# Second recurrence: the small levels and the diagonal as 32x32 squares in four column groups, the 64-token level copied whole

## The reference, cut to what matters

```python
def step(state, inp):
    q_n, k_n, i_n, b_n = inp
    dec = jnp.exp(jnp.where(incl, b_n[:, :, :, None, :] - b_n[:, :, None, :, :], -jnp.inf))
    att = jnp.einsum('bhtd,bhsd,bhtsd->bhts', q_n, k_n, dec)
    o = (jnp.einsum('bhtd,bhdv->bhtv', q_n * jnp.exp(b_n), state)
         + jnp.einsum('bhts,bhsv->bhtv', att, i_n))
    ...
o_hf = _hgrn2_scan(qh, outs[0][0], ih, outs[0][1])
o_hb = _flip(_hgrn2_scan(_flip(qh), _flip(outs[1][0]), _flip(ih), _flip(outs[1][1])))
```

## Time and profile before

| | |
|---|---|
| time, three runs | 1533.93, 1534.42, 1536.74 us; median 1534.42 |
| span of the profiled execution, first to last instruction | 1535.2 us |
| busy: PE, PEld, DVE, ACT | 1508.5, 1403.2, 1200.7, 1015.8 us |
| share of the span: PE, DVE, ACT | 98%, 78%, 66% |
| chain that ended last: PE, DVE, ACT | 84%, 10%, 4% |
| mixer stretches in question | 122 to 182 us and 575 to 636 us |

### The profile page before, as it was taken

One profiled execution on the slowest core, in us unless ns is written; L12 is line 12 of the kernel. 1 busy time (PEld: TensorE's weight loads), 2 busy tenths in 40 slices (PEclk: granted clock), 3 DMA queues, 4 the chain that ended last, 5 costly groups with the idle time before them and its releaser, 6 DMA issues.

```text
span 1535.2 us, 29830 instructions
## 1 busy us (share of the span) xinstructions
PE 1508.5 (98%) x12702; PEld 1403.2 (91%) x12702; DVE 1200.7 (78%) x1693; ACT 1015.8 (66%) x1566; POOL 8.3 (1%) x18
## 2 busy tenths in 40 slices
PE   8999999999999999999999999999999998999998
PEld 8899999988889999999988889968999897899997
DVE  7999766889758799667898768875888578688864
ACT  7786865667646776765776546685777457677753
POOL 0000000000000000000000000000000001000000
PEclk9999999999999999999999999999999999999999
DMA  7522135555554422244655546402655543255551
GB/s 290 192 89 107 56 138 193 200 187 193 207 177 158 158 98 85 84 166 165 236 193 182 212 165 249 155 2 85 218 193 187 193 144 135 83 202 187 190 192 55
DMA packets 35700, 245.55 MB, mean 160 GB/s; under 512 B 4208, under 2 KB 4592, under 8 KB 6512
## 3 DMA queue, kind: packets, MB, share of 16 engines
q1 hardware_dynamic: 35568, 243.65, 44.3%
HBM read 242.58 MB, written 1.05 MB: 159 GB/s over the span
## 4 chain that ended last, share of the span: by engine, by line
PE 84%; DVE 10%; ACT 4%; DMA 1%; issue 1%; SPq 0%; DVEq 0%; ACTq 0%
PE PS L420 83%; DVE WL L1984 2%; DVE SB L1993 1%; DVE SB L1984 1%; DVE SA L1984 1%; ACT WH L1237 1%; ACT SB L1234 1%; DMA RAW<-w_in 1%; PE PS L423 1%; ACT SB L1911 1%; DVE SB L2259 1%; DVE SA L1993 0%; DVE SA L2161 0%; DMA X<-xt 0%; DVE SM L1984 0%
## 5 line engine op out<-in xcount | busy, mean ns | idle before, releaser
L420 PE MATMUL PS<-XHL,WH 128*128 128x256 f32 (+2 forms) x4080 | 846.8, 300 | 6.2 <-DVE WL L1984 3.5
L420 PEld LDWEIGHTS PS<-XHL,WH 128*128 128x128 f32 (+1 forms) x4080 | 644.8, 187 | 43.1 <-issue 5.6
L420 PE MATMUL PS<-XHL,WL 128*128 128x256 f32 (+1 forms) x2392 | 669.5, 280 | 0.0
L1237 ACT CAST WH<-RAW 128x2048 fp32r<-128x2048 f32 (+1 forms) x235 | 427.4, 1822 | 270.8 <-PE PS L420 259.0
L1984 DVE TENSOR_TENSOR WL<-RAW,WH 128x2048 fp32r<-128x2048 f32 (+1 forms) x235 | 511.9, 2181 | 113.2 <-ACT WH L1237 109.4
L420 PEld LDWEIGHTS PS<-XHL,WL 128*128 128x128 f32 (+1 forms) x2392 | 448.3, 187 | 0.4
L420 PE MATMUL PS<-INHL,WH 128*128 128x512 f32 (+1 forms) x1216 | 334.2, 344 | 0.0
L420 PE MATMUL PS<-INHL,WL 128*128 128x256 f32 x960 | 270.0, 281 | 0.0
L420 PEld LDWEIGHTS PS<-INHL,WH 128*128 128x128 f32 x1216 | 210.0, 188 | 27.6
L420 PEld LDWEIGHTS PS<-INHL,WL 128*128 128x128 f32 x960 | 181.2, 189 | 0.0
L1984 DVE TENSOR_TENSOR SB<-SB 128x512 f32<-128x512 f32 (+2 forms) x162 | 108.8, 674 | 14.5 <-ACT SB L1234 11.4
(11 more groups left out here) (156 smaller groups left out, 1446.0 us busy)
## 6 DMA issues: line engine op xcount, KB each, us to landing
RAW<-w_in SPq DMA_DIRECT2D x51, 1024.0 KB, 4.8
RAW<-w_up SPq DMA_DIRECT2D x44, 1024.0 KB, 4.8
RAW<-f_in SPq DMA_DIRECT2D x44, 1024.0 KB, 4.7
RAW<-w_down SPq DMA_DIRECT2D x22, 1024.0 KB, 4.8
RAW<-f_out SPq DMA_DIRECT2D x22, 1024.0 KB, 4.7
RAW<-a_w_in SPq DMA_DIRECT2D x10, 1024.0 KB, 5.0
RAW<-w_out SPq DMA_DIRECT2D x8, 1024.0 KB, 4.8
RAW<-w_bdn SPq DMA_DIRECT2D x4, 1024.0 KB, 4.8
```

The lines of the kernel that those rows point to most:

```text
L420: return e.matmul(out, l, r, start=start, stop=stop, skip_group_check=True)
L1237: e.copy(out, x).then_inc(*A.up(*key, of=of))
```

## The change: what it does

For levels 0 to 4 (g = 1 to 5) and for the diagonal, PE makes the four diagonal 32x32 squares of each unit in place of two 64x64 squares: 32 matmuls, 32 keys by 32 queries, to the four quarters of the PSUM partitions in turn (four column groups), in 256 columns of the bank. `attc` becomes 128x256. The masks of these levels are taken from a second place in the mask table. Level 5 (g = 6) is no longer merged under a mask by DVE: ACT copies its 64x64 squares whole from PSUM into `att`, waits for these copies, and then writes the four quarters of `attc` over the 32x32 squares on their diagonal.

```diff
-        attc = SB[:, 7168:7680].rearrange("p (m n) -> p m n", m=8)
+        attc = SB[:, 7168:7424].rearrange("p (m n) -> p m n", m=8)
+        def quarter_mask(lv):
+            return MKv[:, 2, lv, 64:96].unsqueeze(1).to_broadcast([128, 8, 32])
+        def own_quarter(q):
+            return attq[QUART[q], :, 0:4:3, QUART[q]]
...
                         h, s = divmod(m, 2)
+                        if lv < 5:
+                            for q in QUART:
+                                last = mm(p[q, m * 32:m * 32 + 32], zk[:, h, s, q], zq[:, h, s, q], True, True)
+                            continue
                         for b in range(2):
                             o = HALF[1 - b if lv == 6 else b]
...
-                        for o in HALF:
-                            last = mm(p[o, m * 64:m * 64 + 64], zv[:, h, s, o], qv[:, h, s, o], True, True)
+                        for q in QUART:
+                            last = mm(p[q, m * 32:m * 32 + 32], zv[:, h, s, q], qv[:, h, s, q], True, True)
...
-                    cp(attc, units(ps[st, "hgd"][:, :]), "diag", st, of=ps.out(st, "hgd"))
+                    cp(attc, units(ps[st, "hgd"][:, 0:256]), "diag", st, of=ps.out(st, "hgd"))
...
-                    w.wait_ge(*V["att", st])
+                    w.wait_ge(*P["ps", st, "hg", 6, 1])
                     for b in range(2):
-                        cp(own_square(b, b), heads(attc[HALF[b]]), "att", st)
+                        cp(own_square(b, b), heads(units(ps[st, "hg", 6, 1][:, :])[HALF[b]]), "squares", st, of=ps.out(st, "hg", 6, 1))
+                    waits(A["squares", st], V["att", st])
+                    for q in range(4):
+                        cp(own_quarter(q), heads(attc[QUART[q]]), "att", st)
...
-                    cpred(attc, level_mask(2, HGI[2 * g][1]), units(ps[st, "hg", g, 1][:, :]), "att", st, of=ps.out(st, "hg", g, 1))
+                    cpred(attc, quarter_mask(HGI[2 * g][1]), units(ps[st, "hg", g, 1][:, 0:256]), "att", st, of=ps.out(st, "hg", g, 1))
...
-                kept(6, after=5)
```

More of the change, by code:

```diff
@@ L289, in program @@
         HALF = (slice(0, 64), slice(64, 128))
+        QUART = [slice(32 * j, 32 * j + 32) for j in range(4)]
         att = SB[:, 11264:13312]
@@ L373, in program @@
         KKv = KK.rearrange("p (g n t) -> p g n t", g=4, n=2)
-        QUART = [slice(32 * j, 32 * j + 32) for j in range(4)]
         W2, MV = SA[:, 9472:9984], SA[:, 9984:10496]
@@ L3058, in constants @@
     r, c = np.arange(128)[:, None], np.arange(512)[None, :]
+    quarter = [mk[q:q + 32, 2, 0:5, q:q + 32].copy() for q in range(0, 128, 32)]
     for kind in range(3):
@@ L3061, in constants @@
             mk[64 * b:64 * b + 64, kind, :, 0:64] = mk[64 * b:64 * b + 64, kind, :, 64 * b:64 * b + 64]
+    for q in range(4):
+        mk[32 * q:32 * q + 32, 2, 0:5, 64:96] = quarter[q]
     mv = (r // 16 == 2 * (c // 128) + c % 128 // 64) & (r % 16 < 15)
```

## The result

The changed kernel takes 1537.36 us, the kernel before 1535.51 us in the same series (medians of 20 runs each): ratio 1.0014, interval 1.0008 to 1.0021. That is inside the 0.2% that the prediction called no change, but it is a loss of about 2 us where a gain of 0.4 was forecast, and just above the range. One run of the changed kernel took 5109.71 us and is not in the ratio. The two profiled executions have spans of 1535.2 and 1535.0 us all the same: in that of the kernel before the clock was granted at 0.51 from 988.4 to 995.4 us, outside the mixers, and in the other at 1.00; from 1290.4 to 1300.8 us it is the other way round, 0.84 and 0.51. So the loss has to be read in the mixers. There it is plain: `o_hg` of the second mixer starts 2.65 us later than before (635.94 against 633.29).

The account below looks back on a forecast made before the run. PE bounds the kernel, with DVE arriving together with it in the mixers. Per mixer 1.05 us gained less 0.86 of ACT's tail, 0.38 in all: span 1534.8, less 0.8 for the runs' median, 1534.1 us; range 1532.0 to 1537.0.

Parts of the forecast that it names:

- Where PE's saving stops: Sets g = 1 to 5 could save 2.2 us, but g = 6 waits for DVE's hg_mul, so only 1.05 arrives.
- The sets on PE: Each set's 64 records run in four column groups at once, taking 0.51 us, 0.44 less; six sets a mixer.
- two at once: Only two column groups run side by side in PE's sets: 0.6 us more a mixer, 1535.6 us; chance 0.15.
- as dear as 64 columns: PE's 32-column records cost what 64 columns do, four groups at once: sets unchanged, 1534.9 us; chance 0.08.
- The pace of records stays at 30 ns: PE's sets keep 30 ns a record, each of g = 1 to 5 adding 0.97 us: 1545.8 us; chance 0.12.
- DVE: kept for g = 1 to 5 is 0.27 us shorter each, a 0.23 wait goes: 1.04 earlier at hg_mul's end.
- ACT's tail: squares_out grows by 1.60 us, making hg_last 1.35 later; 0.49 is covered before o_hg, 0.86 a mixer is not.
- The sum: Per mixer 1.05 us gained less 0.86 lost, 0.19 net; 0.38 us over both mixers.
- hg for g = 6 starts when hg_mul has ended, with idle time before it: Sign of a right forecast: PE sits idle before the g = 6 set until DVE's hg_mul ends; no size given.

Follow-up runs that it names:

- e4: Kernel before, with squares_out writing its four 32-row quarters a second time (four more 32x256 copies on ACT); ratio to the kernel before 1.0008, 0.9999 to 1.0017.
- e1: Changed kernel with ACT's two copies of the g = 6 square moved from the head of squares_out to behind dn_z6; ratio to the kernel before 1.0003.
- e13: Changed kernel with early g = 6 copies and half the matmuls in sets g = 1 to 5, leaving two heads' squares out; ratio to kernel before 0.9985.
- e3: Changed kernel with matmuls of hg(1) to hg(5) reordered so two column groups run side by side instead of four; ratio 1.0020, 1.0011 to 1.0029.
- e11: Changed kernel with the first half of the next gate's projection (24 matmuls) moved ahead of o_hg(0) on PE; ratio to the kernel before 1.0002.
- e7: Changed kernel with the diagonal's set issued nine times in the first mixer, 576 records of 32x32 in a row; no ratio given, bursts 3.45 us apart.

## Why the prediction was wrong

From the start of `hg(1)` to that of `o_hg`, in us, first and second mixer:

| kernel | first | second |
|---|---|---|
| before | 32.31 | 32.42 |
| tail alone on the kernel before (e4) | 33.25 | 33.51 |
| changed | 33.82 | 33.43 |
| changed, copies of g = 6 early (e1) | 32.92 | 32.44 |
| changed, early copies, half sets (e13) | 31.22 | 31.23 |

The second mixer's rows for it, `hg(1)` before, then `hg(1)` and `o_hg` of the changed kernel (the earlier trace rows has `o_hg` before):

```profile
600.87 1.15 PE L420 MATMUL PS<-SA 128*64 128x64 f32 x32
```

```profile
602.51 0.76 PE L427 MATMUL PS<-SA 128*32 128x32 f32 x64
...
635.94 1.99 PE L427 MATMUL PS<-SB,SA 128*128 128x256 f32 x8 [0.69 <-ACT SB L1248]
```

- **The step that failed is "Where PE's saving stops".** It let everything from `hg(6)` on be earlier by 1.05 us. `hg_mul` for g = 6 was 0.41 later. The working priced 64 records by the array alone; it did not ask whether twice the records in half the time can be supplied, and so put that wait at nothing: it is 2.10 us in the first mixer and 1.36 in the second. In the kernel before, a row of 160 records of 64x64 steps lasts from 142.50 to 147.43 without a stall, 128 of them 3.9 us; the stretch from 150.00 to 153.29 holds 128 records in 3.29 us with 0.30 of it a stall. Against the 3.3 to 3.8 us between stalls one piece apart the kernel before was close to the edge, and no stall in its trace shows that.
- **The sets on PE: right.** Four groups do run at once, 9 ns a record where 8 were forecast, and a set saves 0.32 to 0.38 us on PE, stalls left out, where 0.44 were forecast; "two at once" and "as dear as 64 columns" fall. The rule of the Trainium skill, TensorEngine Tiling (Array Packing), Performance Considerations, which would have 32 columns cost what 64 do, is not borne out here: a record takes 4 x 9 = 36 ns in its group, against 59 of before.
- **"The pace of records stays at 30 ns" was the rival nearest to what happened**, for a reason that it did not have. From `hg(1)` to the projection behind `hg(2)` takes 154.55 - 147.43 = 7.12 us before and 155.47 - 147.42 = 8.05 after: the two sets with their stalls cost 0.47 more each, where the rival said 0.97 and the forecast 0.44 less.
- **DVE: right in its terms**: 0.43 to 0.45 for `kept`, the wait of 0.23 gone, and without stalls 1.14 arrive where 1.05 were forecast. e13 halves the array's time of a set too, so not all of its gain need be the stalls'; that array time matters little is what e3 shows. Against e1, which has the stalls, e13 is 1.70 and 1.21 us earlier at `o_hg`.
- **ACT's tail: right.** `squares_out` takes 2.9 us (176.60 to 178.29 + 1.68, less 0.47 for `solved(1, 1)`, which stands alone in e1, 176.63 to 177.10); 0.86 was uncovered by the sum, and the runs give 0.94 and 1.09 (e4 against before) or 0.90 and 0.99 (changed against e1).
- **The sum.** Forecast a mixer: 1.05 gained, 0.86 lost. Measured: no gain up to DVE but 0.41 lost in the first mixer and 0.12 in the second, and about 1 us of tail in each: 1.51 and 1.01 later at `o_hg`, 2.5 us in all, inside the 1.2 to 3.2 us of the interval. The base was off as well: the forecast counts from the median of three runs, 1534.42, and the series of 20 gives 1535.51. So of the 3.3 us between 1534.1 and 1537.36 about 1.1 are the base; the range shifted by as much would take the result in, with the mechanism wrong all the same. Nor is a run's time 0.8 us below its span, as the forecast took it: in the series it is 1.8 above, so the profiled execution was a long one.
- **"hg for g = 6 starts when hg_mul has ended, with idle time before it"**: not so in the changed kernel, where PE was late itself; `hg(5)` and `hg(6)` share one row that begins at 167.35 with no idle time.

No version of mine beats the kernel before with all of its work done; the best two, e11 and e1, equal it. Open is what starts a packet. The stalls last 0.2 to 2.4 us; their size goes by when the packet begins and how much of the old piece is left then, and neither was tried by itself.

## What to carry to other kernels

Cutting matmuls into smaller ones raised the pace of records here from one in 30 ns to one in 9 and doubled their number, and the array's time was then not the price: count how many records PE starts in any row of some 128, and compare with the fastest steady stretch that the trace shows without idle time. A stall in the middle of a step, put to issue and on a fixed grid of records, is the mark of it; shifting the stream by half a piece tests it. Filling a stall with other work helps only if nobody waits for what stands behind the filling.

## What the runs showed of the hardware

- PE's instructions came 128 records (256 instructions with the loads) at a time, one packet of 0.02 MB each (103 packets for 13086 records). With nothing but 32x32 records PE used one piece in 3.45 us, at the 1.2 GHz level (e7). At 45 stalls PE went on 2.2 to 2.9 us after a packet had begun.
- Records of 32 columns in four column groups start every 9 ns, against 30 ns for 64x64 in two, both at a granted clock of 1.00.
- In e7 (one run) the granted clock was 1.00 during the first 190 records, 0.92 in the 2.42 us without instructions behind them, and 0.50, the 1.2 GHz level, from 126.73 on; a burst of 128 then took 1.94 us. After 64x64 steps without a stall from 137.62 on it was 0.65 from 142 to 144 us and 1.00 from 144 on.
